# A two-block network on one core: block 0 multiplied as loaded, context loaded and normed later, rounding and low parts reordered

## The reference, cut to what matters

```python
sh1, sc1, ... = split(silu(c) @ ada_w[0] + ada_b[0])          # x; the same with c_ctx for the context
h_l = rmsnorm(x,   norm1_g[0]) * (1 + sc1)  + sh1             # 256 x 1024
h_c = rmsnorm(ctx, norm1_g[0]) * (1 + csc1) + csh1            # 256 x 1024
p_lat, p_ctx = h_l @ w_in, h_c @ w_in                         # w_in: 1024 x 2208
# columns of p: q rank 384 | kv rank 256 | rope 32 | b_gate 512 | c_gate 512 | u 512
# of the context only the kv rank and rope columns are needed here
q  = rmsnorm(p_lat[:, :384]) @ w_uq;   kv = rmsnorm(p[:, 384:640]) @ w_ukv
conv: y = conv3(c_gate * u);  s_l = b_gate * y
```

## Time and profile before

| | before |
|---|---|
| median of 3 runs | 1765.15 us (1765.08 to 1770.49) |
| profiled execution | 1765.0 us, span 1763.2 us |
| TensorE busy | 1627.8 us, 92% |
| VectorE, ScalarE, GpSimd busy | 750.8, 439.6, 125.3 us |
| HBM read | 584.00 MB, 332 GB/s over the span |
| chain that ended last | TensorE 77%, transfers 15%, VectorE 4% |

### The profile page before, as it was taken

The page is one execution under the profiler, slowest core; times in us unless marked ns, Lnnn a source line. Parts: engine busy times, 40 slices in busy tenths (PEclk is TensorE's granted clock), DMA queues, the critical chain, the costliest instruction groups (busy, mean ns, idle before and its releaser), DMA issues.

```text
span 1763.2 us, 21693 instructions
## 1 busy us (share of the span) xinstructions
PE 1627.8 (92%) x8392; PEld 983.6 (56%) x8392; DVE 750.8 (43%) x1182; ACT 439.6 (25%) x692; POOL 125.3 (7%) x151
## 2 busy tenths in 40 slices
PE   6999889999999999999999999999959897899776
PEld 2964678888878888876334443344413342344222
DVE  5577588777478886653222221122201120112012
ACT  3535554543445443342000000000000000000001
POOL 1942010000500000020000000000000000000000
PEclk8999999999999999999999999999989898999989
DMA  9634469885468877528999999999999999999995
GB/s 383 225 107 167 156 238 333 297 320 177 166 256 309 324 285 271 195 89 313 400 427 426 426 426 427 426 424 427 426 426 425 425 428 417 424 426 426 427 426 206
DMA packets 80891, 586.31 MB, mean 333 GB/s; under 512 B 9856, under 2 KB 11136, under 8 KB 48544
## 3 DMA queue, kind: packets, MB, share of 16 engines
q1 hardware_dynamic: 80800, 585.08, 83.0%
HBM read 584.00 MB, written 1.05 MB: 332 GB/s over the span
## 4 chain that ended last, share of the span: by engine, by line
PE 77%; DMA 15%; DVE 4%; issue 1%; SPq 1%; ACT 1%; DVEq 0%; ACTq 0%
PE psum L1327 23%; PE psum L1342 10%; DMA mraw<-dn_dram 4%; DMA mlast<-gu_dram 4%; PE psum L974 4%; PE psum L976 4%; PE psum L975 4%; PE psum L1092 3%; PE psum L1300 3%; PE psum L995 2%; PE psum L997 2%; PE psum L996 2%; PE psum L1355 2%; DMA araw<-ada_dram 2%; DMA mlast<-dn_dram 2%; PE psum L787 2%
## 5 line engine op out<-in xcount | busy, mean ns | idle before, releaser
L1327 PE MATMUL psum<-mraw,xsat 128*64 128x512 f32 (+2 forms) x1560 | 407.4, 628 | 50.7 <-DMA mraw<-gu_dram 25.9
L1327 PEld LDWEIGHTS psum<-mraw,xsat 128*64 128x64 f32 (+2 forms) x1560 | 136.6, 142 | 274.3 <-issue 273.7
L1342 PE MATMUL psum<-mraw,xsat 128*64 128x512 f32 (+2 forms) x664 | 181.1, 615 | 16.6 <-DMA mraw<-dn_dram 10.2
L1327 PE MATMUL psum<-mlast,xsat 128*64 128x512 f32 (+2 forms) x352 | 137.4, 614 | 11.7 <-DMA mraw<-gu_dram 11.7
L974 PE MATMUL psum<-wh,ah 128*128 128x512 f32 x352 | 139.4, 396 | 3.5 <-DVE al L2019 2.6
L1905 POOL TENSOR_TENSOR wl<-raw,wh 128x256 fp32r<-128x256 f32 x132 | 114.2, 902 | 366.3 <-DVE work L2046 216.8
L975 PE MATMUL psum<-wl,ah 128*128 128x512 f32 x352 | 137.3, 390 | 0.0
L976 PE MATMUL psum<-wh,al 128*128 128x512 f32 x352 | 137.3, 390 | 0.0
L2560 DVE TENSOR_TENSOR oacc<-psum,oacc 128x512 f32<-128x512 f32 x60 | 38.7, 686 | 218.0 <-PE psum L1355 218.0
L1342 PE MATMUL psum<-mlast,xsat 128*64 128x512 f32 (+2 forms) x320 | 122.0, 605 | 0.0
L2067 DVE TENSOR_TENSOR wl<-raw,wh 128x1024 fp32r<-128x1024 f32 x88 | 104.8, 1232 | 30.0 <-ACT wh L1609 29.9
(11 more groups left out here) (389 smaller groups left out, 2541.7 us busy)
## 6 DMA issues: line engine op xcount, KB each, us to landing
mraw<-gu_dram SPq DMA_DIRECT2D x83, 2048.0 KB, 21.8
mraw<-dn_dram SPq DMA_DIRECT2D x37, 2048.0 KB, 25.4
araw<-ada_dram SPq DMA_DIRECT2D x128, 512.0 KB, 4.8
raw<-ffa_dram SPq DMA_DIRECT2D x44, 1024.0 KB, 5.0
mlast<-gu_dram SPq DMA_DIRECT2D x20, 2048.0 KB, 20.6
mlast<-dn_dram SPq DMA_DIRECT2D x18, 2048.0 KB, 29.3
mraw<-gu_dram SPq DMA_DIRECT2D x29, 1024.0 KB, 16.2
raw<-ffb_dram SPq DMA_DIRECT2D x44, 512.0 KB, 5.2
```

What stands on the lines that cost most here:

```text
L1327: last = mm(ps[4 + n][a * w:(a + 1) * w, :], xs[:, k * P + a * w:k * P + (a + 1) * w], slot_columns(slot, n * 512), start=False, stop=(k = ...
L1342: last = mm(ps[n][a * w:(a + 1) * w, :], at[:, k * P + a * w:k * P + (a + 1) * w], slot_columns(slot, i * D + n * 512), start=(k == 0), st ...
```

## The change

- The blocks of b_gate come first (0 to 3), then the q rank (4 to 6); the rest keeps its place.
- Block 0 is multiplied in plain float32 from the loaded weights and from `work` (8 products), with no rounding and no low part. `s_hi` and `s_lo` 1 are given by a table load on ScalarE and a clearing on VectorE at the start. Block 5's load, which reuses block 0's slot, also waits for `s_blk` 1.
- SyncE loads the context behind blocks 0 to 2, after the sum of x's squares.
- The norm of x is alone at the start (256-column squares, sums, root). VectorE scales all eight chunks first, then makes all low parts (`first_norm`); the copy of block 0 stands between low parts 5 and 6.
- ScalarE rounds blocks 1 and 2, then the chunks of x, then blocks 3 and 4, then squares the context.
- VectorE makes block 3's low part (768 and 256 columns). GpSimd makes 1, 2 and from 4 on; its last piece of block 4 waits for block 3's.
- The context's squares are added by VectorE behind blocks 0 to 2, summed by TensorE behind block 3; root on ScalarE before block 6's rounding; VectorE scales by gain and reciprocal in one operation behind blocks 3 and 4, and makes the low parts behind blocks 4 to 6. ScalarE has one operation a chunk.
- The eight modulation steps on VectorE move from behind blocks 4 to 11 to behind 7 to 14.
- TensorE issues 3 products of `keep_clock` behind each of pairs 2 to 6 and 2 behind pair 7, and 2 in place of 5 before block 0.

```diff
@@ -39,7 +39,7 @@
...
-B_Q, B_CB, B_KV, B_KPE, B_CC, B_CU = 0, 3, 7, 9, 10, 14
+B_CB, B_Q, B_KV, B_KPE, B_CC, B_CU = 0, 4, 7, 9, 10, 14
@@ -453,6 +453,8 @@
...
+                if b == NFIRST_RAW:
+                    sp.wait_ge(s_blk, 1)
@@ -478,13 +480,14 @@
...
             sp.dma_start(x[:, :, :], xT_d).then_inc(s_xin, 16)
-            sp.dma_start(xc[:, :], xc_d).then_inc(s_xin, 16)
...
                 blk(b)
+            sp.wait_ge(s_sum, 1)
+            sp.dma_start(xc[:, :], xc_d).then_inc(s_xin, 16)
@@ -794,26 +797,37 @@
...
             pe.wait_ge(s_sqx, 7)
-            mm(ps[3][:, :], ones, work[:, 0, :], start=True, stop=True).then_inc(s_sum, 1)
+            mm(ps[3][:, 0:T], ones, work[:, 0, 0:T], start=True, stop=True).then_inc(s_sum, 1)
...
                 ada_rows(k)
+                keep_clock(3)
             row_columns(0)
-            for k in range(6, 8):
-                ada_rows(k)
+            ada_rows(6)
+            keep_clock(3)
+            ada_rows(7)
+            keep_clock(2)
...
-            keep_clock(5)
+            keep_clock(2)
+            pe.wait_ge(s_raw[0], RAW_LOADED[0])
+            for j in range(DJ):
+                pe.wait_ge(s_h, j + 1)
+                last = mm(ps[0][:, 0:T], raw[:, j * P:(j + 1) * P], work[:, j, 0:T], start=(j == 0), stop=(j == DJ - 1))
+            last.then_inc(s_blk, 1)
             rot = cone[NOPE:QD, _E["rot"]:_E["rot"] + ROPE]
-            for b in range(B_O):
-                block_product(b, 2 * T if B_KV <= b <= B_KPE else T, fresh={0: (s_hl, 0), B_KV: (s_hlx, 0)}.get(b))
+            for b in range(1, B_O):
+                block_product(b, 2 * T if B_KV <= b <= B_KPE else T, fresh={1: (s_hl, 0), B_KV: (s_hlx, 0)}.get(b))
+                if b == 3:
+                    pe.wait_ge(s_ntx, 1)
+                    mm(ps[3][:, T:2 * T], ones, work[:, 0, T:2 * T], start=True, stop=True).then_inc(s_cqsum, 1)
...
                     for j in range(3):
-                        pe.wait_ge(s_cqs, j + 1)
+                        pe.wait_ge(s_cqs, DJ + j + 1)
...
                     for j in range(2):
-                        pe.wait_ge(s_cqs, 4 + j)
+                        pe.wait_ge(s_cqs, DJ + 4 + j)
@@ -1491,11 +1505,11 @@
...
-            act.wait_ge(s_xin, 32)
+            A(warm[:, :], V("eps", 0, 1), ACT.Sqrt).then_inc(s_hi, 1)
+            act.wait_ge(s_xin, 16)
...
-                A(work[:, j, 0:T], x[:, j, :], ACT.Square)
-                A(work[:, j, T:2 * T], xc[:, j * TC:(j + 1) * TC], ACT.Square).then_inc(s_sq, 1)
-            norm_root(0, 2 * T)
+                norm_square(0, j)
+            norm_root(0)
@@ -1503,26 +1517,35 @@
...
             ada_row(1)
-            for b in range(3):
+            for b in (1, 2):
...
             h_hi(0)
+            for b in (3, 4):
+                block_hi(b)
+            act.wait_ge(s_xin, 32)
+            for j in range(DJ):
+                A(work[:, j, T:2 * T], xc[:, j * TC:(j + 1) * TC], ACT.Square).then_inc(s_cqs, 1)
             def ctx_hi(j):
-                act.wait_ge(s_ntx, j + 1)
-                link(A(work[:, j, T:2 * T], work[:, j, T:2 * T], ACT.Identity, bias=modx[:, j:j + 1], scale=gsx[:, j:j + 1]))
-                A(ah3[:, j, T:2 * T], work[:, j, T:2 * T], ACT.Copy).then_inc(s_hhx, 1)
...
-            for b in range(3, 7):
+                act.wait_ge(s_ntx, j + 2)
+                A(ah3[:, j, T:2 * T], work[:, j, T:2 * T], ACT.Identity, bias=modx[:, j:j + 1]).then_inc(s_hhx, 1)
...
+            block_hi(5)
+            act.wait_ge(s_cqsum, 1)
+            A(rt[:, T:2 * T], ps[3][:, T:2 * T], ACT.Sqrt, bias=V("eps"), scale=1.0 / D).then_inc(s_cqrt, 1)
+            block_hi(6)
+            for j in range(4):
+                ctx_hi(j)
+            block_hi(7)
+            for j in range(4, DJ):
+                ctx_hi(j)
+            block_hi(8)
+            for j in range(3):
+                act.wait_ge(s_ev, B_Q + j + 1)
+                A(sqf[:, j * T:(j + 1) * T], cq[:, j, :], ACT.Square).then_inc(s_cqs, 1)
+            for b in range(9, 11):
                 block_hi(b)
-                ctx_hi(2 * (b - 3))
-                ctx_hi(2 * (b - 3) + 1)
-            block_hi(7)
-            for j in range(3):
-                act.wait_ge(s_ev, j + 1)
-                A(sqf[:, j * T:(j + 1) * T], cq[:, j, :], ACT.Square).then_inc(s_cqs, 1)
-            for b in range(8, 11):
-                block_hi(b)
-            act.wait_ge(s_cqsum, 1)
+            act.wait_ge(s_cqsum, 2)
@@ -1908,12 +1931,14 @@
...
                 for q in range(0, D, PIECE):
+                    if b == 4 and q == D - PIECE:
+                        pool.wait_ge(s_lo, 4)
...
             pool.wait_ge(s_lo, 1)
-            for b in range(1, B_F):
+            for b in (1, 2) + tuple(range(4, B_F)):
@@ -1978,8 +2003,8 @@
...
-                TTn(modx[:, 0:16], both[:, :, 1], two, ALU.add)
-                TTn(mod[:, 0:16], both[:, :, 0], two, ALU.add).then_inc(s_mod, 2)
+                TTn(mod[:, 0:16], both[:, :, 0], two, ALU.add).then_inc(s_mod, 1)
+                TTn(modx[:, 0:16], both[:, :, 1], two, ALU.add).then_inc(s_mod, 1)
@@ -2054,10 +2068,48 @@
...
+            def first_norm():
+                dve.wait_ge(s_rt, 1)
+                link(V_.reciprocal(rstd[:, 0:T], rt[:, 0:T]))
+                for j in range(DJ):
+                    TTn(work[:, j, 0:T], x[:, j, :], rstd[:, 0:T], ALU.mult).then_inc(s_nt, 1)
+                first_mods()
+                norm_gain(_V["n1"], 0)
+                for j in range(DJ):
+                    dve.wait_ge(s_nt, j + 1)
+                    TS(work[:, j, 0:T], work[:, j, 0:T], gs[:, j:j + 1], m_col(0, j), ALU.mult, ALU.add).then_inc(s_h, 1)
+                for j in range(DJ):
+                    dve.wait_ge(s_hh, j + 1)
+                    TTn(al3[:, j, 0:T], work[:, j, 0:T], f32(ah3[:, j, 0:T]), ALU.subtract).then_inc(s_hl, 1)
+                    if j == 5:
+                        evacuate(0, cbg[:, 0, :])
+                dve.wait_ge(s_hi, 3 + 1)
+                TTn(wl[:, SPLIT[3] * D:SPLIT[3] * D + 768], raw[:, RAW[3]:RAW[3] + 768],
+                    f32(wh[:, SPLIT[3] * D:SPLIT[3] * D + 768]), ALU.subtract)
+                dve.wait_ge(s_lo, 3)
+                TTn(wl[:, SPLIT[3] * D + 768:(SPLIT[3] + 1) * D], raw[:, RAW[3] + 768:RAW[3] + D],
+                    f32(wh[:, SPLIT[3] * D + 768:(SPLIT[3] + 1) * D]), ALU.subtract).then_inc(s_lo, 1)
+                dve.wait_ge(s_mod, 2)
+                link(STT(gsx[:, :], modx[:, 8:16], 1.0, vec[:, _V["n1"]:_V["n1"] + 8], ALU.add, ALU.mult))
...
+            def ctx_sum(part):
+                for j in part:
+                    dve.wait_ge(s_cqs, j + 1)
+                    ins = TTn(work[:, 0, T:2 * T], work[:, 0, T:2 * T], work[:, j, T:2 * T], ALU.add)
+                    if j < DJ - 1:
+                        link(ins)
+                    else:
+                        ins.then_inc(s_ntx, 1)
...
+            def ctx_scaled(part):
+                for j in part:
+                    STT(work[:, j, T:2 * T], xc[:, j * TC:(j + 1) * TC], gsx[:, j:j + 1], rstd[:, T:2 * T], ALU.mult, ALU.mult
+                        ).then_inc(s_ntx, 1)
...
-                TTn(al3[:, k, T:2 * T], work[:, k, T:2 * T], f32(ah3[:, k, T:2 * T]), ALU.subtract).then_inc(s_hlx, 1)
+                STT(al3[:, k, T:2 * T], work[:, k, T:2 * T], modx[:, k:k + 1], f32(ah3[:, k, T:2 * T]), ALU.add, ALU.subtract
+                    ).then_inc(s_hlx, 1)
@@ -2088,21 +2140,25 @@
...
+            V_.memset(kgone[NOPE:QD, :], 1.0).then_inc(s_lo, 1)
...
-                TTn(work[:, 0, :], work[:, 0, :], work[:, j, :], ALU.add).then_inc(s_sqx, 1)
-            norm(0, _V["n1"], 0, hl=0)
+                TTn(work[:, 0, 0:T], work[:, 0, 0:T], work[:, j, 0:T], ALU.add).then_inc(s_sqx, 1)
+            first_norm()
...
-                if b < B_CB:
-                    evacuate(b, cq[:, b, :])
+                if b == 0:
+                    pass
+                elif b < B_Q:
+                    evacuate(b, cbg[:, b - B_CB, :])
...
-                    evacuate(b, cbg[:, b - B_CB, :])
+                    dve.wait_ge(s_ntx, b - B_Q + 2)
+                    evacuate(b, cq[:, b - B_Q, :])
@@ -2112,18 +2168,28 @@
...
                     TTn(czp[:, b - B_CU, 1:T + 1], ps[b % 2][:, 0:T], ccg[:, b - B_CU, :], ALU.mult).then_inc(s_ev, 1)
-                if b < 4:
-                    ctx_lo(2 * b)
-                    ctx_lo(2 * b + 1)
-                elif b < 12:
-                    ada(ADA_FIRST + b - 4)
+                if b in (0, 1, 2):
+                    ctx_sum(((1, 2), (3, 4), (5, 6, 7))[b])
+                elif b == 3:
+                    dve.wait_ge(s_cqrt, 1)
+                    link(V_.reciprocal(rstd[:, T:2 * T], rt[:, T:2 * T]))
+                    ctx_scaled(range(4))
+                elif b == 4:
+                    ctx_scaled(range(4, DJ))
+                    ctx_lo(0)
+                    ctx_lo(1)
```

(12 more changed lines are left out.)

## The result

| | before | after |
|---|---|---|
| median (17 runs each) | 1765.39 us (1761.69 to 1770.76) | 1772.83 us (1770.16 to 1776.15) |
| ratio | | 1.0035, 95% interval 1.0028 to 1.0043 |
| profiled execution | 1765.0, span 1763.2 | 1776.15, span 1774.1 |
| TensorE: block 1 starts | 45.59 | 39.74 |
| block 7 (first wide one) starts | 62.87 | 61.62 |

The kernel became slower by 0.35%, 6.2 us (4.9 to 7.6 by the interval). I had forecast 1762.6 with a range up to 1767.0, so the sign and the range were both wrong. In the profiled executions the loss is made between block 7 and the columns behind block 17: 43.14 us before, 49.04 after, 5.90 more. The front did gain, but 1.25 us of the forecast 2.4 by block 7.

What follows compares the result with a forecast made beforehand. TensorE was taken to bound the kernel, so only an earlier dense stream pays. Block 7 at 60.5 instead of 62.87 gains 2.4 us, nothing lost behind it: 1762.6 us, main case 1761 to 1764, 8-in-10 range 1758.0 to 1767.0.

Steps and rivals of the forecast that it cites:

- Part 1 and 2: Start of kernel: context loaded later lands pair 7 2.56 us earlier; fillers leave 1.0 of it, modulation at 34.3, not 36.77.
- the rival on the clock: Second turning into columns: clock falls, turning takes 3.6 us, not 1.95; block 0 issued at 43.9, whole 1766; chance 0.16.
- Part 3 and 4: Scaling of x and block 0: first chunk at 34.75, block 0 issued by 40.4 against 45.59, 5.2 us earlier.
- Part 5: Block 0 to block 7: VectorE's added work stalls TensorE; block 7 at 60.5 against 62.87, 2.4 us left.
- The three stalls: TensorE waits before block 3 (0.6 us), before the context's sum (0.8) and before block 7 (1.0).
- Part 6: Behind block 7: later modulation steps delay loads of blocks 12 to 17; priced at 0, with 0 to 1.5 us lost.
- late modulation steps decide: Rival behind block 14: late loads lose 2.2 us of a front gain of 2.4 to 4; whole 1764.5; chance 0.10.
- That a shift reaches the end: Behind block 7: no wait on absolute time, so the 2.4 us reach the end; the contrary rival, 1765, had 0.04.

Runs made afterwards that it cites:

- the first experiment: The changed kernel with SyncE's queue alone reordered, so that loads of blocks 12 to 17 no longer stand behind loads waiting for modulation steps: 1765.98 us, ratio 1.0004.
- less work in blocks 16 and 17: Changed kernel with loads reordered, roundings ahead, GpSimd's wait and block 3 on GpSimd; blocks 16 and 17 keep only high x high products: 1765.41 us, ratio 0.9993.
- the steps paired: The changed kernel with two modulation steps behind each of wide blocks 7, 8 and 9, and one behind 10 and 11: 1768.86 us, ratio 1.0016.

## Why the prediction was wrong, point by point

**Part 1 and 2, front.** The pair-7 product ended at about 30.5, not 31.45, and the modulation came at 33.37, not 34.3. TensorE works without a pause from 15.2 on, 2.6 us for a pair and its fillers, which is what a pair takes to land: the products of pairs 3 to 5 begin 0.04 us behind their landings. The queue appears with the first turning. Pair 7 landed at 27.95 (28.3 by my sum) and its product began at 29.53, so the queue was 1.6 us and not 2.3. The fillers are on the path from there, as I said; but the clock was up at 15.2, not at 20.5. That early rise is partly luck of this execution: the product at that place took 1.06 to 1.94 us in the ten executions with these fillers, and the next one, at 17.6 to 19.5, about 1.07 in all of them. The kernel before had taken its first product in that stretch at 19.19, and I carried its 5 us over to a TensorE that was busy earlier. Without fillers the turning takes 3.57: the rival on the clock was right about what they guard against, and was not what happened.

**Part 3 and 4, scaling.** Eight chunks in 5.44 us, from 33.78. I had six at 0.73 and two at 0.34, from 34.75. Block 1 started at 39.74, forecast 40.4. Right in mechanism. That it came 0.7 sooner is no better sum but the clock's early rise: with the same front other executions have 39.70 to 41.15, and 40.4 lies in their midst.

**Part 5, to block 7.** The three stalls are where I put them. The first two measured about 0.84 and 0.87 (forecast 0.6 and 0.8), the third 1.76 (forecast 1.0), with 0.3 at block 6 that I had not. Together 3.8 against 2.4, so that block 7 was at 61.62 in place of 60.5. The term most mis-sized is the last: ScalarE began block 7's rounding at 56.89 (56.45 by my sum), and GpSimd's four pieces ran from 58.01 to 61.6 (3.0 us by my sum, 3.6 measured). Rounding ahead of the context gave 59.98.

**Part 6, behind block 7.** This is the step that failed: "I put 0 here, with 0 to 1.5 lost". The measured loss is 5.9: block loads that stood behind modulation loads landed late, ScalarE and GpSimd stood still for them, and TensorE for both. Three things were wrong in it.
- I took the load of block 17 as asked at 92.2 and landing at 96, that is 3.8, where the earlier trace rows have 3.4 to 5.0 and 4.2 in the middle. In the kernel before, too, block 17's load (83.73) has a modulation load 0.42 us ahead of it, and it took 4.6; block 16's took 4.8. The row of SyncE that I had passed over:

```profile
83.31 0.33 SPq L449 DMA_DIRECT2D araw<-ada_dram  x1
```

In after all six have one, and the first four landed in 4.8 to 5.3 us. The last two block loads and their modulation loads are asked for 2.8 and 3.3 us behind the pair ahead of them, before that one is in; these block loads took 6.4 and 7.0. Block 17's was asked for at 93.8 and was there at 100.9.
- I worked out only the last block. Block 16 was asked at 90.5 and its low part was done 12.0 us later. The sum made for block 17 (7.8 to 8.3 us for the same way) already had no room, at 100.5 for 100.7.
- I looked at GpSimd and not at what stands behind the waiting instruction on ScalarE: the kv squares, 0.9 to 1.2 us lost with no block in it. And a gap of 2.2 us cost another 1.7 by the clock.

The rival *late modulation steps decide* had the mechanism, and named it: "each load behind block 14 comes late". I gave it 0.10 and 2.2 us; the gaps alone are 4.3 and the clock another 1.7. Moving only the steps, and repairing only the loads' order, showed that it is the cause.

**That a shift reaches the end.** "I see no such wait." For a delay it held: 3.1 us put in behind block 17 gave 2.7 at the mixer. For an advance it didn't, in any of four kernels. I had looked for waits on absolute time and found none, but didn't look at how the later stages are paced: by loads of modulation chunks of 4.3 to 5.3 us on the chain, where TensorE's work was cut by 15.4 us with 1.9 gained (some 10 us of that to the clock). So had Part 6 been 0, the time would probably have been near 1765 to 1766, as the first experiment's was, and not the forecast 1762.6.

**What is left open.** The stage's end explains 4.65 of the 6.2 us; the interval leaves 0.3 to 3.0. In the profiled execution the shift grows to 5.6 by the mixer and more in the expert stage, where the clock falls at other places in each execution. Whether advances are lost in general, and why, is open beyond the cases shown.

## What to carry to other kernels

When a step is moved that frees a buffer, write down for every load that stands behind it in the issuing queue when it will be asked for, when it lands (by the duration of a load that has as much asked for just ahead of it), and which engine's queue stands behind its landing; a margin of 0.2 us for the last one is no margin for the others. Queue order and step places must be changed together: either one alone put the columns 4 to 5 us late here (and the whole 4.1 and 2.3 us), both together not. And before pricing a gain at the front of a long kernel, ask the chain of waits of the later stages whether TensorE paces them; a delay passes where an advance may not.

## What the runs showed of the hardware

- **A VectorE step can be shut out for many GpSimd pieces in a row.** A two-input step of 1,024 columns that takes 1.3 us took 9.23 while GpSimd ran 28 pieces of 0.75 without a gap; the same steps were back to 1.57 in the mean once GpSimd paused for them. The Trainium skill (SBUF — State Buffer, SBUF: two separate sides) says that whichever starts first has the shared port pair for its whole instruction and the other fully blocks. The run agrees, and adds that the one blocked did not get in between two pieces of the other.
- **The granted clock can fall behind a gap of about 2 us, and then costs about as much again or more.** By start-to-start distances, in after it fell 1.5 us behind a gap of 2.2 (1.7 us lost), with only the steps moved 0.9 behind one of 2.16 (1.7 lost), and with less work in blocks 16 and 17 2.1 behind one of 2.1 (3.4 lost); it did not fall behind one of 2.4 with the steps paired, nor behind the one of 1.9 at block 7 in after. So a gap on TensorE is to be priced at its length and, perhaps, as much again.
- **A load's time to land goes by what was asked for just ahead of it.** In the kernel before, from 62 us on, 512 KB took 3.2 to 3.8 us with nothing asked for in the 2.3 us ahead (four loads), and 4.6 and 4.8 with another 512 KB asked for 0.42 us ahead; with one asked for 2.05 ahead it took 5.0. In after it took 4.8 to 5.3 with one 0.42 ahead (four loads), and 6.4 and 7.0 where such pairs followed each other by 2.8 and 3.3 us.
